# A wait for each score map in attention, and identity products in TensorE's waits elsewhere

## What is computed

```
y_b = merge_heads(global_gqa(qB, [kB, kBc], [vB, vBc]))                    # 4 heads, 768 keys
y_c = merge_heads(diff_attention(qC, [kC, kCc], [vC, vCc], lam, ...))      # 4 heads, 2 softmax maps each
y_d = merge_heads(window_gqa_latent(qD, kD, vD, kDc, vDc, wn_sink))        # a window, the context and a sink
y = concat([y_a, y_b, y_c, y_d]) * silu(g)
x_new = layer_norm(alpha * x + gate * (y @ w_out), ln_g, ln_b)
```

```
o = g0 * attention(q, k_cmp, v_cmp) + g1 * attention(q, selected) + g2 * attention(q, window)
mixed = sum_n sigmoid(xn @ w_gate + b_gate)[n] * (ys[n] @ w_branch[n])
x = x + mixed @ w_out
x = x + square(relu(rms(x) @ w_mlp1)) @ w_mlp2
```

## Time and profile before

| | us |
|---|---|
| median of 3 timed runs (2225.24 to 2228.26) | 2226.21 |
| profiled execution, its own time | 2222.2 |
| its span, first to last instruction | 2220.3 |
| TensorE busy in the span | 2029.4 |
| VectorE busy | 1137.2 |
| ScalarE busy | 755.5 |
| mean granted TensorE clock, share of full speed | 0.968 |

### The profile page before, as it was taken

How to read it: one execution, slowest core, us unless ns; L and a number is a source line. 1 busy time by engine, 2 the same in 40 slices (tenths; PEclk the granted TensorE clock), 3 DMA queues, 4 the chain that set the end, 5 groups by cost and what they waited for, 6 DMA issues and landing times.

```text
span 2220.3 us, 26204 instructions
## 1 busy us (share of the span) xinstructions
PE 2029.4 (91%) x9904; PEld 1374.2 (62%) x9904; DVE 1137.2 (51%) x2482; ACT 755.5 (34%) x1621; POOL 54.3 (2%) x96
## 2 busy tenths in 40 slices
PE   6989999899779999998888879998899997999999
PEld 2565465445444465564455437885688876887887
DVE  1664145655654947125666567977444434333333
ACT  2132133554441123123554324326332224222222
POOL 2000000000010000000000110000000000000000
PEclk9999999999989999999999888998999998999999
DMA  8111010002361211121000242221233331333331
GB/s 290 39 48 38 29 57 29 10 1 77 135 211 48 69 48 38 52 72 39 1 1 11 87 97 69 84 77 30 58 97 102 95 100 53 95 95 95 95 95 67
DMA packets 152684, 157.27 MB, mean 71 GB/s; under 512 B 5676, under 2 KB 114384, under 8 KB 152560
## 3 DMA queue, kind: packets, MB, share of 16 engines
q1 hardware_dynamic: 146672, 137.91, 20.5%
q0 software_dynamic: 5888, 17.68, 2.8%
HBM read 151.37 MB, written 4.19 MB: 70 GB/s over the span
## 4 chain that ended last, share of the span: by engine, by line
PE 72%; DVE 18%; ACT 5%; issue 4%; DMA 1%; POOL 0%; ACTq 0%; DVEq 0%; POOLq 0%
PE psum L752 15%; PE psum L1208 10%; PE psum L1209 10%; PE psum L1210 9%; PE psum L936 5%; PE psum L780 5%; PE psum L764 5%; DVE stats L2037 3%; PE psum L969 2%; PE psum L950 2%; PE psum L713 2%; ACT arena L1488 2%; DVE arena L2303 2%; PE psum L798 1%; ACT arena L1314 1%
## 5 line engine op out<-in xcount | busy, mean ns | idle before, releaser
L752 PE MATMUL psum<-arena 128*128 128x512 f32 (+1 forms) x1280 | 459.5, 515 | 0.8 <-ACTq L1317 0.8
L1314 ACT ACTIVATE arena<-psum 128x256 f32<-128x256 f32 (+6 forms) x520 | 205.2, 423 | 671.4 <-PE psum L713 212.1
L1208 PE MATMUL psum<-part,part 128*128 128x512 f32 x992 | 392.6, 396 | 14.8 <-DVE part L2422 7.0
L1209 PE MATMUL psum<-part,part 128*128 128x512 f32 x992 | 391.5, 395 | 0.0
L1210 PE MATMUL psum<-part,part 128*128 128x512 f32 x992 | 391.2, 394 | 0.0
L752 PEld LDWEIGHTS psum<-arena 128*128 128x128 f32 x1280 | 239.5, 191 | 193.3 <-issue 177.2
L2418 DVE TENSOR_TENSOR part<-arena,part 128x1024 fp32r<-128x1024 f32 x112 | 137.1, 1226 | 251.9 <-ACT part L1314 251.9
L1314 ACT ACTIVATE part<-arena 128x1024 fp32r<-128x1024 f32 (+1 forms) x198 | 174.2, 913 | 219.9 <-PE psum L1210 149.8
L1208 PEld LDWEIGHTS psum<-part,part 128*128 128x128 f32 x992 | 189.2, 191 | 57.4 <-issue 13.9
L2037 DVE TENSOR_REDUCE stats<-psum 128x1 f32<-128x768 f32 (+6 forms) x208 | 138.8, 709 | 151.0 <-PE psum L936 149.6
L1210 PEld LDWEIGHTS psum<-part,part 128*128 128x128 f32 x992 | 189.2, 191 | 40.6
(11 more groups left out here) (269 smaller groups left out, 2001.2 us busy)
## 6 DMA issues: line engine op xcount, KB each, us to landing
arena<-in_w_in SPq DMA_DIRECT2D x75, 512.0 KB, 4.2
arena<-in_w_mlp SPq DMA_DIRECT2D x64, 512.0 KB, 3.9
arena<-in_w_ada SPq DMA_DIRECT2D x48, 512.0 KB, 5.6
arena<-in_w_gate SPq DMA_DIRECT2D x32, 512.0 KB, 4.0
arena<-in_w_out SPq DMA_DIRECT2D x24, 512.0 KB, 3.8
arena<-in_w_in SPq DMA_DIRECT2D x16, 256.0 KB, 3.2
arena<-in_w_branch SPq DMA_DIRECT2D x8, 512.0 KB, 4.8
arena<-in_x POOLq DMA_DIRECT2D x4, 512.0 KB, 9.0
```

Source lines behind the costliest of these rows:

```text
L752: mm = pe.matmul(bank(b)[:, c0:c1], lhs[:, k, m * P:(m + 1) * P], ring.view(tag, l, k // 2)[:, k % 2, c0:c1], start=k == 0, stop=k == kt - 1)
L1208: pe.matmul(dst, lo, x_hi_, start=first, stop=False)
L1209: pe.matmul(dst, hi, x_lo_, start=False, stop=False)
L1314: return act.activation(dst, src, ACT.Copy)
```

## The change

Three edits. First, `scores` opens map 1's banks only behind map 0's first product, and raises a counter for each map; `row_max` waits for map 0 and map 1 one by one. In masked steps both waits come before the masks of that map. Second, ScalarE's wait for an old step's scores names map 1's counter. Third, a helper `keep_going(b, n)` writes n products of the identity with itself (128 x 128, float32) into bank b, and it is called at twelve places, behind the `open_bank` and ahead of the wait for the data (for `mlp1` behind the wait for weights). Nothing reads what these products write; the real product overwrites it.

```diff
+            def keep_going(b, n):
+                for _ in range(n):
+                    pe.matmul(bank(b)[:, 0:P], ident[:], ident[:], start=True, stop=True)
...  scores
-                for j in range(2):
-                    open_bank(map_bank(l, k, j))
-                for c0, rhs in segments:
-                    for j in range(2 if rhs.shape[-1] else 0):
+                segments = [(c0, rhs) for c0, rhs in segments if rhs.shape[-1]]
+                for n_segment, (c0, rhs) in enumerate(segments):
+                    for j in range(2):
+                        if n_segment == 0:
+                            open_bank(map_bank(l, k, j))
                         mm = pe.matmul(...)
-                mm.then_inc(att_mm(("s", l, k)), 1)
+                        if n_segment == len(segments) - 1:
+                            mm.then_inc(att_mm(("s", l, k, j)), 1)
...  attend, l == 2, first round, ahead of scores
+                        keep_going(map_bank(l, 0, 0), 4)
...  turn_y, half 0 of m == 0
+                            keep_going(b, 12)
...  layer_end, first of the gate products
+                            keep_going(2, 5)
...  rms_turned
+                        if half == 0:
+                            keep_going(b, ((0, 14, 28, 4), (0, 13, 13, 4))[which][m])
...  feature_mm, i == 2
+                    keep_going(b, 6)
...  compressed_2, p == 11
+                    keep_going(2, 9)
...  product_wide, at its start
+                open_bank(0)
+                keep_going(0, 8)
...  mixing, d == 0 and n == 0
+                            keep_going(b, 11)
...  mixing, branch product of d == 0
+                        keep_going(2, 9)
...  hidden_layer, f == 0
+                        keep_going(b, 7)
...  row_max
-                dve.wait_ge(*att_mm.at("s", l, k))
-                for j in range(2):
+                for j in range(2 if masks else 0):
+                    dve.wait_ge(*att_mm.at("s", l, k, j))
                     for c0, n, mask in masks:
...
                 for j in range(2):
+                    if not masks:
+                        dve.wait_ge(*att_mm.at("s", l, k, j))
                     dve.reduce_max(col[:, j:j + 1], score_map(l, k, j)[:, lo:hi], AX, negate=True)
```

More of the change, by code:

```diff
@@ L988, in attend @@
                         prepare(l, i + 2, banks)
+                    if l == 2 and i == 0:
+                        open_bank(map_bank(l, 0, 0))
+                        keep_going(map_bank(l, 0, 0), 4)
                     if i < len(steps_):
@@ L1006, in turn_y @@
                     if half == 0:
+                        if m == 0:
+                            keep_going(b, 12)
                         pe.wait_ge(*gy_dve.at("y", l, m))
@@ L1017, in layer_end @@
                         open_bank(2 + half)
+                        if v == 0 and half == 0:
+                            keep_going(2, 5)
                         pe.wait_ge(*bc_dve.at("diag", l, v, half))
@@ L1068, in feature_mm @@
                 hi, lo = parts_2(("fm", i))
+                if i == 2:
+                    keep_going(b, 6)
                 for k in range(KT):
@@ L1248, in mixing @@
                         open_bank(b)
+                        if d == 0 and n == 0:
+                            keep_going(b, 11)
                         pe.wait_ge(*lo_dve.at(("gate", d, n)))
@@ L1256, in mixing @@
                     if d == 0:
+                        open_bank(2)
+                        keep_going(2, 9)
                         pe.wait_ge(*xlo_dve.at("y", KT - 1))
@@ L1275, in hidden_layer @@
                     pe.wait_ge(*lo_dve.at(("mlp1", f)))
+                    if f == 0:
+                        keep_going(b, 7)
                     for k in range(KT):
@@ L1475, in prepare @@
                 if n >= 2:
-                    act.wait_ge(*att_mm.at("s", l, [j for j in range(k) if tile_number(l, j) == n - 2][-1]))
+                    act.wait_ge(*att_mm.at("s", l, [j for j in range(k) if tile_number(l, j) == n - 2][-1], 1))
                 act.activation((queries_t_2 if l == 2 else queries_t)[:, n % 2, :], bank(banks["q", n])[:, 0:256], ACT.Copy,
```

## The result

| | us | ratio to before, 95% |
|---|---|---|
| before, beside it (4 runs, 2224.2 to 2228.26) | 2225.72 | |
| changed (4 runs, 2208.29 to 2212.34) | 2210.08 | 0.9927 (0.9913 to 0.9941) |

The change makes the kernel 15.6 us faster. The time lies in the range that I gave, near its slow end; the gain is half of the 32 that I forecast. The profiled execution took 2211.09 us, 11.1 less than the one of before (2222.2).

A forecast was written before the change was run, and what follows sets the result against it. TensorE, with 72% of the chain, was taken as the bound, through its work at low clock and its waits; 16 from attention and 16.1 from identity products took 2222.2 to 2190.2, plus 4.0 for timed runs: 2194 us, range 2180 to 2212.

The forecast's parts named there:

- Scores and maxima: First two attentions: map 0's scores and maximum no longer wait for map 1's exponential; 16 us less, ends 0 and 24.
- 32 waits x 0.54: Scores waiting for exponentials: each of 32 waits shortens by 0.54 us, 17.3 in all, taken as 16.
- All later links of the loop move by the same amount: Attention's loop of scores, maxima and exponentials: everything behind map 0's maximum starts earlier by the same 0.54 us.
- My overtaking end (24): Attention scores: map 0's short product ends before map 1's long one, maximum 0.9 to 1.0 us earlier, 24 us in all.
- Identity products: Twelve places outside the score loop: filling TensorE's waits holds the clock at full speed behind them; 16.1 us less.
- `mlp2`: 8 identity products in a 2.06 us wait, 3.00 us of low-clock work behind it; gain 1.6, called among the surest.
- `turn_y` and gate, both layers: 12 and 5 identity products, 2.6 us left for 2.56; possible overrun 1.5, gain 0.9 per layer, 1.8 in all.
- `out2`: 8 identity products in a 2.67 us wait, 5.40 us of low-clock work behind it; gain 2.7, called among the surest.
- third attention: First step of l = 2: four identity products, 13 us at low clock behind; 3.5 if the clock holds, doubted, taken 1.0.
- Attention gives nothing: Rival: copies' waits and TensorE's own list eat the earlier maximum; 16 us less only, 2210 us; chance 0.17.
- Clock not held: Rival: identity products are issued but the clock falls as before, costing 12.4 us; 2222.6 us, no change; chance 0.10.
- the overrun rival: Rival: identity products overrun the waits of both norms and `turn_y` by 12.4 us, attention giving under 8; slower, to 2239; chance 0.06.

The follow-up runs named there:

- `map0_whole`: Changed kernel with both of map 0's score products ahead of map 1's bank opening and products: 2210.91 us, 0.9929 of the kernel before.
- `no_out2`: Changed kernel without the 8 identity products ahead of the out2 product: 2210.83 us, 0.9927 of the kernel before.
- `maps_only`: Changed kernel without its identity products, scores and maxima by map kept: 2215.94 us, 0.9956 of the kernel before.
- `identity_only`: Changed kernel with the kernel before's order of scores and maxima, identity products kept: 2217.01 us, 0.9960 of the kernel before.
- `tuned`: Changed kernel without out2's 8 identity products, with 14 more in layer 1's attention and 7 at the third's first waits: 2207.48 us, 0.9914 of before.
- `no_l2`: Changed kernel without the four identity products ahead of the third attention's first scores: 2207.98 us, 0.9924 of the kernel before.
- the short list: Half of the gate's products beside attention left out of the changed kernel: 2208.99 us (0.9931) with the old score order, 2193.12 us (0.9858) with the new.

## Why the prediction was right in sign and half in size

**Scores and maxima, forecast 16, measured 8.5 alone and 6.9 beside the identity products.** What the edit does is as I said: map 0's first product no longer waits for exponential 1, and the maximum is 0.42 earlier in a step that waited (0.54 forecast). The term that was mis-sized is "32 waits x 0.54", for three reasons that the traces show.

First, "All later links of the loop move by the same amount" is wrong. The loop that I wrote down left out ScalarE's copy of turned weights, which stands ahead of exponential 0 and ended 0.08 before it already in the trace of before. Exponential 0 moves 0.19 for the maximum's 0.42, and the step 0.29. `map0_whole` gives a 0.40 earlier maximum and changes no step. Second, an earlier maximum shortens the step behind it, and only if its own burst began early. In the tile shown one of the two waits lies behind a burst that did not, and its step gained 0.12. Third, the steps behind them are TensorE's own list and give nothing, as I had said; with the list shortened more of them gain. Per tile it is 0.41 and not 1.08. The 6.9 compares medians of two groups of runs; by each kernel's distance from the kernel before beside it, it is 8.2. I also wrote that half the steps show no wait, but with 32 waits in 104 steps it is more than two thirds. My overtaking end (24) was out of reach by the same copy, and not for the reason that I named.

**Identity products, forecast 16.1, measured 7.5 alone and 5.9 beside the maps.** By the shift of the same records from the trace of before to that of the changed kernel, each place measured from just ahead of it to just behind the low-clock work that it had:

| place | forecast | trace |
|---|---|---|
| first norm and `feature_mm` | 3.0 | 3.4 |
| second norm and `mlp1` | 3.8 | 4.1 |
| `mixing` | 2.2 | 2.9 |
| `mlp2` | 1.6 | 1.6 |
| `turn_y` and gate, both layers | 1.8 | 0.8 |
| `out2` | 2.7 | -0.5 |
| third attention | 1.0 | -3.0 |

The sum of the last column is 9.3. The price (0.213 a product) and the claim that they hold the clock stand. Two terms failed. For `out2` I took a wait by its size and its line from the earlier trace rows and did not ask to which pair of the loop it belonged: `keep_going` stands at the start of `product_wide`, the wait ahead of its last pair, 35 us on. The eight cost 1.8; the 1.3 that the last pair's stretch gave back came in `no_out2` too, without them. I had called this term one of the two surest. In the third attention four products don't hold the clock, as I doubted, and 3.0 are lost. It is neither part alone: from first to last score the stage took 53.0 us before, 52.6 in `maps_only` and in `identity_only`, and 55.6 to 58.5 in all the profiles that have both parts without the seven products of `tuned`, `no_l2` among them. Why both together do it stays open. `turn_y` was the overrun that I described: the twelve took most of 4.47 us, in part at the low clock, in a wait of 2.6, and the window's 0.83 instead of 0.50 paid for that.

**The rivals.** "Attention gives nothing" names 2210, which is the time that came, but not what happened: attention gave half, and so did the rest. "Clock not held" and the overrun rival are out, by the windows at 1.00 behind both norms, `mixing` and `mlp2`. What the Trainium skill says of transposes ("TensorE: Matmul & The Clock Gate", Part 4: PE-mode transpose) is left untested, for these are ordinary products; no run here puts transposes in their place.

**What stays open.** In layer 1 the clock is low for 20 to 44 us in the new order, and in the old one for 17, 20 and (with the short list) 44. Two executions of one kernel give 34 and 20, and first to last score 179.0 and 170.8, while the attention of layer 0 took 239.3 and 245.8. So the place at which the clock falls moves from one execution to the next and shifts up to 8 us between stages. I can't say how much of the 8.5 would be more without it, and the 22 steps that were at low clock in one profile or the other are not accounted for.

## What to carry to other kernels

An earlier link moves the next one only if nothing else stands ahead of that one in its engine's list: write down the whole list of each engine in the loop, small copies too. An engine's wait is worth at most the distance to the next bound of the same loop: before multiplying a gain by the number of waits, write down each step's period and what each engine's own list takes, and cap the gain step by step. A view of waits does not show waits inside a burst, so measure steps from the end of one burst to the end of the next. Before filling a wait, find the iteration in which it stands, and not only its line. Filler work that opens a bank early brings that bank's reader into the list; put it where the bank is known to be free.

## What the runs showed of the hardware

Products in different rows of the array do pass each other, while their signals keep the order of the list. In `map0_whole` map 1's first product stands behind both of map 0's. In a step without a wait, all that TensorE does for the scores between 442.32 and 442.50:
```profile
442.31 0.71 PE L941 MATMUL psum<-arena 32*128 32x512 f32 x2
```
These are the first 512-column records of map 0 and of map 1, which start at 442.31 and 442.33. Map 0's second product starts only at 443.27, so map 1's has started 0.95 ahead of a product that stands before it in the list.

The signal is another matter. In the changed kernel's step above, map 1's first product stands between map 0's two. Map 0's second one runs from 433.96 to 434.55, inside map 1's first, which ends at 434.94 (ends of products are modelled in the profile); yet the maximum, which waits for map 0 alone, starts at 434.99. In `map0_whole`, with no product of map 1 ahead of it, map 0's last product ends as long after the burst's start (1.55 in both), and the maximum starts 0.40 earlier. The Trainium skill ("TensorE: Matmul & The Clock Gate", Part 3, The mechanism) has products strictly in order in start and end. The counters here agree with that, and so did the 0.42; the starts of the records do not, and there the measurement decides.

A TensorE that the page shows as busy need not have the full clock: in layer 1 of `maps_only` it is busy for 51.03 of 56 us at a mean granted clock of 0.70, with score products that use 32 rows, and it stays at half clock for up to 10.2 us at a stretch there. The second profile of the changed kernel was busy for 51.22 at 0.91. Waits inside bursts count as busy in both, and no run here tells what decides between the two.
